# Projection tiles of a hybrid attention and mLSTM block computed in another order

## The reference, cut to what matters

```
h = rms_norm(x, mix_norm_w)
proj = h @ w_in
aq, ak, av, iq, ik, iw, mq, mk, mv, mi, mf, mo = split(proj)
# indexer: which 256 keys each query may see, for every block of 128 queries
idx_score = einsum('bqh,bqhs->bqs', wi, relu(einsum('bqhd,bsd->bqhs', qi, ki)))
sel = top_k(idx_score masked to earlier chunks, 256)
att_out = softmax(rope(aq) . rope(ak)[sel]) . av[sel]          # 8 heads, 2 key heads
# mLSTM: 4 heads of 128, chunkwise matrix memory
q, k = split(silu(causal_conv4([mq, mk])))
mem_out = norm(mlstm(q, k, mv, mi, log_sigmoid(mf))) * sigmoid(mo)
x = x + concat(att_out, mem_out) @ w_out
x = x + moe(rms_norm(x))                                       # top 4 of 32 experts
out = rms_norm(x)
```

## Time and profile before

| | |
|---|---|
| time, median of 3 runs | 2528.6 us (2527.76 to 2529.83) |
| the profiled execution's own time | 2529.42 us |
| its span, first to last instruction | 2527.6 us |
| PE busy | 2269.2 us (90%) |
| DVE busy | 1806.2 us (71%) |
| ACT busy | 1378.8 us (55%) |
| POOL busy | 520.3 us (21%) |

### The profile page before, as it was taken

The page is one execution under the profiler, slowest core; times in us unless marked ns, Lnnn a source line. Parts: engine busy times, 40 slices in busy tenths (PEclk is TensorE's granted clock), DMA queues, the critical chain, the costliest instruction groups (busy, mean ns, idle before and its releaser), DMA issues.

```text
span 2527.6 us, 41675 instructions
## 1 busy us (share of the span) xinstructions
PE 2269.2 (90%) x15519; PEld 1799.5 (71%) x15519; DVE 1806.2 (71%) x2070; ACT 1378.8 (55%) x1547; POOL 520.3 (21%) x455
## 2 busy tenths in 40 slices
PE   5689999757997949999999999999999999999994
PEld 4567788656886747777777777777777777777773
DVE  3589999904434378778778778678777777777885
ACT  3362223555653246666566566566666666656665
POOL 1006786670002001111110110111111111101020
PEclk9899999767998969999999999999999999999997
DMA  5011111001003338888798897898888888879887
GB/s 131 17 34 34 51 50 52 12 21 67 1 2 123 119 136 306 285 311 300 278 319 306 270 325 279 293 319 284 299 310 287 307 291 302 309 283 314 308 314 276
DMA packets 253391, 525.95 MB, mean 208 GB/s; under 512 B 32969, under 2 KB 59721, under 8 KB 252973
## 3 DMA queue, kind: packets, MB, share of 16 engines
q1 hardware_dynamic: 240204, 483.27, 53.8%
q0 software_dynamic: 13120, 41.82, 6.4%
HBM read 490.44 MB, written 35.91 MB: 208 GB/s over the span
## 4 chain that ended last, share of the span: by engine, by line
PE 72%; DMA 9%; DVE 6%; ACT 5%; issue 4%; POOL 2%; SPq 1%; POOLq 0%; ACTq 0%; DVEq 0%
PE ps L1701 13%; PE ps L1702 12%; PE ps L1703 12%; PE ps L1708 6%; PE ps L1400 6%; PE ps L1401 6%; PE ps L1402 6%; DMA xg<-h_d,gcur 5%; DMA e_raw<-in_w_gate_up_dram 3%; PE ps L1579 2%; PE ps L1713 1%; PE ps L1691 1%; PE ps L1570 1%; PE ps L1752 1%; DVE score L1921 1%
## 5 line engine op out<-in xcount | busy, mean ns | idle before, releaser
L2208 DVE TENSOR_TENSOR e_wlo<-e_raw,e_whi 128x2048 fp32r<-128x2048 f32 x410 | 925.3, 2284 | 143.8 <-ACT e_whi L1283 142.4
L1283 ACT ACTIVATE e_whi<-e_raw 128x2048 fp32r<-128x2048 f32 x411 | 783.6, 1915 | 371.0 <-PE ps L1703 212.2
L1701 PE MATMUL ps<-e_whi,xh 128*128 128x512 f32 x1088 | 441.9, 406 | 5.8 <-DVE e_wlo L2208 5.8
L1702 PE MATMUL ps<-e_whi,xl 128*128 128x512 f32 x1088 | 425.6, 391 | 0.0
L1703 PE MATMUL ps<-e_wlo,xh 128*128 128x512 f32 x1088 | 424.8, 390 | 0.0
L933 POOL DMA_INDIRECT x_d<-ym,scur x34 | 72.1, 2121 | 942.8 <-ACT ym L1316 923.1
L1701 PEld LDWEIGHTS ps<-e_whi,xh 128*128 128x128 f32 x1088 | 204.7, 188 | 71.2 <-issue 26.4
L1703 PEld LDWEIGHTS ps<-e_wlo,xh 128*128 128x128 f32 x1088 | 204.8, 188 | 44.9
L1702 PEld LDWEIGHTS ps<-e_whi,xl 128*128 128x128 f32 x1088 | 205.0, 188 | 37.7
L1701 PE MATMUL ps<-e_whi,ath 128*128 128x512 f32 x544 | 226.1, 416 | 6.2 <-DVE atl L2236 4.9
L1703 PE MATMUL ps<-e_wlo,ath 128*128 128x512 f32 x544 | 213.5, 392 | 0.0
(11 more groups left out here) (357 smaller groups left out, 3581.7 us busy)
## 6 DMA issues: line engine op xcount, KB each, us to landing
e_raw<-in_w_gate_up_dram SPq DMA_DIRECT2D x275, 1024.0 KB, 5.2
e_raw<-in_w_down_dram SPq DMA_DIRECT2D x136, 1024.0 KB, 7.8
w_raw<-in_w_in_dram SPq DMA_DIRECT2D x20, 512.0 KB, 3.8
xt<-in_x_dram SPq DMA_DIRECT2D x8, 512.0 KB, 3.5
wo_raw<-in_w_out_dram SPq DMA_DIRECT2D x8, 512.0 KB, 6.6
xr<-in_x_dram SPq DMA_DIRECT2D x8, 512.0 KB, 4.2
x_d<-x SPq DMA_DIRECT2D x8, 512.0 KB, 2.6
h_d<-h SPq DMA_DIRECT2D x8, 512.0 KB, 2.9
```

The lines of the kernel that those rows point to most:

```text
L1283: nc.scalar.activation(e_whi[:, m % HRING, :], e_raw[:, m % RING, :], ACT.Copy).then_inc(s.e_hi, 1)
L1701: nc.tensor.matmul(dst, a_hi, slot_hi, start=False, stop=False, skip_group_check=True)
L1702: nc.tensor.matmul(dst, a_lo, slot_hi, start=False, stop=False, skip_group_check=True)
L2208: nc.vector.tensor_tensor(e_wlo[:, m % HRING, :], e_raw[:, m % RING, :], e_whi[:, m % HRING, :].bitcast(F32), ALU.subtract).then_inc(s.e_l ...
```

## The change

Tiles 0 to 3 stay. The order behind them becomes: 4 to 7 mLSTM values, 8 to 15 convolved queries and keys, 16 to 19 output gates, 20 to 23 attention queries, 24 keys, 25 values.

- PE computes tile 4 behind the indexer's rotary swaps, then transposes the indexer weights, then computes tile 5, and only then begins the score units.
- Tiles 6 and 7 are cut into 16 parts of three matmuls. A part follows each even score unit from unit 8 on, 20 parts in all: the whole of tile 6 and four parts of tile 7. The other 12 parts of tile 7 follow the indexer. Tile 6 is evacuated by ACT behind Relu 42.
- The value tiles' transposes move from banks 0 to 3 to the banks 4 to 7 that held their tile: two in the first score block (behind units 1 and 3), the third behind the indexer, the fourth behind tile 8. A tile's PSUM banks are now also held by its transposes, so tiles 6 to 9 wait for the copies of tiles 4 to 7.
- The convolutions are done four operations to a tile in tiles 10 to 23, as before relative to their own tiles. The rotary turns of the attention tiles now come in POOL's queue at 22 to 26: the first two in front of the last eight convolution operations, the last one behind all tiles, and the attention value tile's evacuation, transposes and copy behind that.
- Buffers are placed anew (`vtmp`, `vmo`, `vwide`, `qtmp`), and SP stores the output gates in between the loads of tiles 19 to 22.

```diff
-FT_IQ, FT_IK, FT_SMALL, FT_Q, FT_K, FT_V, FT_MQK, FT_MV, FT_MO, NFT = 0, 2, 3, 4, 8, 9, 10, 18, 22, 26
+FT_IQ, FT_IK, FT_SMALL, FT_MV, FT_MQK, FT_MO, FT_Q, FT_K, FT_V, NFT = 0, 2, 3, 4, 8, 16, 20, 24, 25, 26
+PARTS = 16
+CONV_EACH = 4
...
# POOL
+                if f == FT_MV + 1:
+                    gp.wait_ge(s.v_gate, 12)
+                    gp.wait_ge(s.v_ra, 3)
+                    nc.gpsimd.memset(mvtok[:, :, :, MD:MD + 1], 1.0).then_inc(s.g_zero, 1)
...
-                if f >= FT_MQK + 2:
-                    for n in range(4 * (f - FT_MQK - 2), 4 * (f - FT_MQK - 1)):
+                if FT_MQK + 2 <= f < NFT:
+                    first = CONV_EACH * (f - FT_MQK - 2)
+                    for n in range(first, min(first + CONV_EACH, 8 * CONV_STEPS)):
                         convolve(n)
...
# ACT, inside the loop over the 48 score units
+                if u == 3:
+                    rows_of_values(0)
+                if u == 5:
+                    rows_of_values(1)
+                if u == 42:
+                    evacuate(FT_MV + 2)
+                    hi(FT_MV + 4)
...
# ACT, in the loop over the later tiles
+                for j in range(8):
+
+                    if FT_MQK + 2 + (CONV_STEPS * j + CONV_STEPS - 1) // CONV_EACH == f:
+                        silu(j)
+                if f <= NFT:
                     evacuate(f - 1)
...
# PE
+                if n == 0:
+                    pe.wait_ge(s.g_wlo, f + 1)
...
+                    if FT_MV + 2 <= f < FT_MQK + 2:
+                        pe.wait_ge(s.a_vt, f - FT_MV - 1)
...
+            project(FT_MV)
             pe.wait_ge(s.a_ev, 4)
             pe.wait_ge(s.v_rm, 3)
             for t in range(NT):
                 m = nc.tensor.transpose(ps[:, 0, t * IH:(t + 1) * IH], iwt[0:IH, t * P:(t + 1) * P], ident[0:IH, 0:IH])
             m.then_inc(s.p_iwt, 1)
+            project(FT_MV + 1)
             pe.wait_ge(s.a_iwt, 1)
             pe.wait_ge(s.v_iqlo, 1)
+            part = 0
...
                 m.then_inc(s.p_is, 1)
+                if u == 1:
+                    value_transposes(0)
+                if u == 3:
+                    value_transposes(1)
+                if u >= 8 and u % 2 == 0:
+                    project_part(FT_MV + 2 + part // PARTS, part % PARTS)
+                    part += 1
...
-            for f in range(4, NFT + 1):
+            value_transposes(2)
+            for f in range(FT_MV + 3, NFT + 1):
                 if f < NFT:
-                    project(f)
+                    project(f, part - PARTS if f == FT_MV + 3 else 0)
+                if f == FT_MQK:
+                    value_transposes(3)
```

More of the change, by code:

```diff
@@ new lines, in _, with iq_hi_of @@
+            hi(0)
+            for f in range(1, FT_MV):
+                hi(f)
+                evacuate(f - 1)
+            hi(FT_MV)
+            evacuate(FT_SMALL)
+            hi(FT_MV + 1)
+            act.wait_ge(s.v_ra, 3)
+            nc.scalar.activation(ik_hi[:], ikt[:], ACT.Copy).then_inc(s.a_iqhi, 1)
+            def iq_hi_of(i):
+                if i == 2:
+                    act.wait_ge(s.g_zero, 1)
+                if i >= 4:
+                    act.wait_ge(s.p_is, IH * (i - 3))
+                for g in range(4):
+                    rows = slice(ID * g, ID * g + ID)
+                    nc.scalar.activation(iq_hi[rows, i % 2, g::4, :], iqt[rows, :, i * P:(i + 1) * P], ACT.Copy).then_inc(s.a_iqhi, 1)
@@ new lines, in _ @@
+            iq_hi_of(2)
+            act.wait_ge(s.p_iwt, 1)
+            nc.scalar.activation(iwc, ps[:, 0, 0:NT * IH].rearrange("p (t h) -> p t h", t=NT), ACT.Copy).then_inc(s.a_iwt, 1)
+            evacuate(FT_MV)
+            hi(FT_MV + 2)
+            evacuate(FT_MV + 1)
+            hi(FT_MV + 3)
+            for u in range(6 * IH):
+                i, h = 2 + u // IH, u % IH
+                w = P * (i + 1)
+                if h == 2 and i + 1 < NT:
+                    iq_hi_of(i + 1)
+                act.wait_ge(s.p_is, u + 1)
+                if u >= 2:
+                    act.wait_ge(s.v_score, 9 * ((u - 2) // IH) + (u - 2) % IH + 1)
+                nc.scalar.activation(rbuf[:, u % 2, 0:w], pair(2 * (u % 2))[:, 0:w], ACT.Relu).then_inc(s.a_relu, 1)
+                if u == 3:
[5 more added lines that the diff above has]
+                    hi(FT_MV + 4)
@@ L1110, in m_chunk @@
+                if f == FT_V + 2:
+                    rows_of_values(4)
             def m_chunk(c):
```

176 lines of the change are left out of this document (77 added, 99 removed).

## The result

The changed kernel takes 2536.8 us (median of 9 runs, 2531.34 to 2543.53), the kernel before in the same session 2528.2 us (2527.14 to 2530.55): a ratio of 1.0034, 95% interval 1.0020 to 1.0047. It is slower, by 8.6 us, where I had said 2526 and most likely no difference; it lies outside my range of 2518.5 to 2535. Both intervals lie above 1, but differences of this size are small beside the spread of the times (2531.34 to 2543.53 above). The profiled execution took 2531.62 us, 5 us under the median; a second profile of the same kernel took 2539.01. I read both.

A forecast was written before the change was run, and what follows sets the result against it. PE was taken to bound the kernel up to the first mLSTM matmul, with some 32 us idle ahead of an all-PE stretch. Items 1 to 7 sum to -4.6, the clock adds +2.1, giving -2.5 us: 2526, range 2518.5 to 2535.

The forecast's parts named there:

- Item 1: Start of the scores, first block: unit 8 on PE at 125.8 instead of 123.2, +2.6 us.
- Item 2: Five score blocks with 20 parts partly filling PE's waits: +6.0 us; plus 0.9 for value transposes behind the indexer.
- the 0.9: One set of value transposes added behind the indexer: +0.9 us of PE work.
- Items 3, 4 and 5: PE work moved off the later tiles: -38.1 us; new wait between tiles 8 and 9, convolutions in tiles 10 to 21: nothing.
- Item 6: Attention tiles: POOL, with rotary turns and convolutions, makes PE wait 2.2, 4.7, 5.8 and 1.7 us: +14.4.
- Item 7: Tail: PE waits 10.8 us for the last turn, evacuations and copies, against 1.15 before: +9.6.
- Item 8: Granted clock falls around PE's waits in the attention tiles and tail: +2.1 us, bounds 0 and 11.
- my own case: Whole kernel: 2526 us, own range 2522 to 2530, with the clock costing +2.1; 56%.
- The second one (2535): PE falls to the low clock in first score block, tile 24 and tail, paying 11.3 us: 2535; chance 11%.
- The first: Score blocks: parts fit fully into PE's waits, blocks grow only +3.2 us, clock costs nothing: 2521; chance 24%.
- the third: POOL falls behind from tile 10 on, 12 tiles 0.9 us longer, +10.8: 2537; chance 7%.
- the fourth: Score blocks: PE alternating between two PSUM bank pairs runs half the time at half rate, +15 us: 2541; chance 2%.

The follow-up runs named there:

- apart: Changed kernel with POOL's low parts of tiles 7 and 8 held behind score additions and tile 6's put before the scores: 2532.9 us, 1.0011 to before.
- portop: Kernel before the change with three POOL operations added beside DVE's score additions, their results unused: 2528.4 us, one run.
- noparts: Changed kernel with no parts of tiles 6 and 7 between score units, both tiles following the indexer: 2542.3 us, 1.0049 to before.
- tail: Changed kernel with the attention value tile's buffer separated from the rotary turns' scratch, so its evacuation need not wait for the last turn: 2525.1 us, 0.9983 to before.
- warm: Changed kernel with nine unused matmuls filling PE's last wait, before the attention values' transposes: 2531.6 us, 1.0008 to before.
- again: Changed kernel run once more without any edit, for a second profile and set of times: 2535.1 us, 1.0019 to before.
- tailapart: Changed kernel with the value tile freed from the last turn and low parts of tiles 7 and 8 kept off the scores: 2527.6 us, 0.9985 to before.
- bestwarm: Changed kernel with separate tail buffers, later low parts, rotary turns on DVE, and two unused matmuls in the last wait: 2510.4 us, 0.9917 to before.

## Why the prediction was wrong, by its own steps

The sum was for the first mLSTM matmul, and said 435.6. Against the two profiles of the changed kernel (us):

| term | predicted | first profile | second |
|---|---|---|---|
| items 1 and 2, to the gates' transposes | +8.6 | +12.0 | +12.4 |
| items 2 (the 0.9), 3, 6, 7 and 8, from there to the instant | -11.1 | -11.8 | -10.0 |
| instant against before | -2.5 | +0.2 | +2.4 |
| first chunk, against 4.9 | 0 (in item 8) | +1.5 | +3.7 |
| `m_kw` to the end | 0 | +0.5 | +3.5 |
| sum | -2.5 | +2.2 | +9.6 |

- **Item 1 failed.** It put the cost of POOL's low parts beside DVE at nothing. The step was "by following the three engines through the eight units I get unit 8 on PE at 125.8 instead of 123.2: +2.6"; Relu 8 came 5.1 later (129.3 against 124.2). I followed DVE's additions at the durations of a trace in which POOL stood idle through the whole indexer (0.00 us of POOL), and the change puts POOL's low parts there. I counted them as time on POOL alone ("its low part is no obstacle"). They cost DVE 1.75 us at the rotary product, 3.4 at the first additions and 1.3 at an addition of 1024 keys in the last block; 3.4 to 3.8 us more than I had reached the gates' transposes. The first of the three did not count against my sum: DVE's first score came at 118.26, 0.7 before my 119.0. `apart` and `portop` show it, from both sides; `apart`, which takes away the second and the third but puts 2.1 us onto a scan and 0.9 onto another addition, gives 3.1 back. The trace before shows no such place in the indexer, but it has one behind the attention, which I did not look for: four low parts on DVE beside four on POOL, then two of the same size on DVE beside a memset of POOL. The Trainium skill (SBUF — State Buffer, "Who interferes with whom") lists this collision: a VectorE instruction with two SBUF inputs contends with a GpSimd instruction that reads SBUF for a shared port pair, which is an exclusive lock, and the order of issue decides which one is blocked. The numbers agree, to 0.1 us: POOL's low part ended at 97.64 + 2.39 = 100.03, and 1.21 behind that is 101.24; the product ended at 101.11. These are the rows of the kernel before (DVE twice, then POOL):

```profile
759.07 12.41 DVE L2023 TENSOR_TENSOR wo_lo<-wo_raw,wo_hi 128x1024 fp32r<-128x1024 f32 x4 [3.27 <-ACT wo_hi L1240]
771.41 2.35 DVE L2028 TENSOR_TENSOR mx_lo<-mixt,mx_hi 128x1024 fp32r<-128x1024 f32 x2
```
```profile
758.17 12.23 POOL L884 TENSOR_TENSOR wo_lo<-wo_raw,wo_hi 128x1024 fp32r<-128x1024 f32 x4 [186.32 <-ACT wo_hi L1240]
```

  Side by side, one takes 3.1 us on DVE and 3.1 on POOL; without the other, 1.2 and 2.4 (240.06 in the earlier trace rows). With these rows the collision could have stood in the prediction as a term or a rival.
- **Item 2** held but for that: from Relu 8 to Relu 47 the blocks grew by 6.9 us, not 6.0, and the last block's low part with its 1.3 is in that. `noparts` shows the parts' gain. (One reading ahead of it was off: the 1.2 us behind the last unit is not one of the ten waits of the earlier trace rows, so nine waits with 10.5 us lay in the blocks. No term changes by it.)
- **Items 3, 4 and 5** held: one wait of 1.3 for `mvtok`, none for a low part in tiles 10 to 21.
- **Item 6** held in mechanism, and in size as a whole. The rows of after, in the order in which I had followed them:

```profile
371.18 1.06 ACT L1054 ACTIVATE mqk<-ctmp 128x1024 f32<-128x1024 f32 x1 [8.50 <-POOL ctmp L770]
372.14 1.01 ACT L1042 ACTIVATE qt<-ps 128x1024 f32<-128x1024 f32 x1
...
373.20 3.67 PE L1540 MATMUL ps<-qt,cst 128*128 128x512 f32 x4 [1.97 <-ACT qt L1042]
...
379.94 0.61 PE L1429 MATMUL ps<-ht_hi,w_hi 128*128 128x512 f32 x1 [3.07 <-POOL w_lo L778]
...
394.34 1.06 ACT L1054 ACTIVATE mqk<-ctmp 128x1024 f32<-128x1024 f32 x1 [16.41 <-POOL ctmp L770]
...
396.37 2.95 PE L1540 MATMUL ps<-qt,cst 128*128 128x512 f32 x4 [3.65 <-ACT qt L1042]
```

  The waits are 2.0, 3.1, 3.7 and 0.5, together 9.2, against my 2.2, 4.7, 5.8 and 1.7, together 14.4. PE's own work filled the rest: a swap that takes 1.76 took 3.67 here, at a low clock. POOL's queue set the time, whatever PE did in it: from the first swap to the third I had 37.8 us, and it is 37.9 in both traces. Behind the third, where PE's own speed counts, tile 24 at the low clock took 0.5 us more than at the full one in the first trace and 2.3 more in the second.
- **Item 7** held: 9.5 us, and `tail` takes 7.5 of them away.
- **Item 8 was mis-sized.** I took +2.1, with bounds 0 and 11. In the tail alone `warm` measures 4.6, where I had "about 1 to 2". I had tied that loss to the 9.6 us of waiting; `tail` shows the first chunk as slow (8.6 us) behind a wait of 2.0. The clock fell in a third place too, which my own case had put at nothing: in the first block, where the low parts made PE wait 1.84 us for a Relu (0.80 and 0.88 in the windows). In `apart` that wait and that low clock are gone together; which brought which is not shown, and waits of up to 1.33 us are left there at a clock of 1.00.
- **The rivals.** The second one (2535) came closest to the medians, at 11%: the clock did fall in all three of its places, but the part of it that I can put a number to (0.5 to 2.3 in tile 24, 2.4 to 4.6 in the tail) is less than its 11.3, and the collision on DVE and POOL, which was no rival of mine, comes with up to 3.8. The first is refuted: it needed the blocks to grow by 3.2 us and the clock to cost nothing, and they grew by 6.9; the third by the missing waits; the fourth by windows of 1.00 with units and parts alternating. Of the signs I had set, the gates' transposes came 12.0 us later and not 8.5, and the first mLSTM matmul at 438.4 and 440.6 and not at 432 to 437. Of the conditions for being wrong, two came true: the clock was under 1.00 between 123 and 370, and in the second profile the work behind the first chunk differs by 3.5 us. The blocks of 512 to 1024 keys by themselves grew by 6.9, so that one did not. The top-k's room is 52.5 us, as expected (about 50 instead of 63.4):

```profile
DVE k_lo L2015 <- ACT k_hi L1227: 52.5, 1, 52.5
```

- **The whole.** Of the 12.1 us between my sum and the second profile (9.6 + 2.5), 3.8 lie up to the gates' transposes, where `apart` and `portop` point to POOL's low parts (with the clock that fell behind them), 1.1 from the rest of the projection, 3.7 from the first chunk at the low clock, and 3.5 from behind it, for which no step of mine and no edit gives a cause. The first profile is off by 4.7: 3.4, -0.7, 1.5 and 0.5. The medians lie between the two.
- **What stays open.** From the first token transposes of the experts to the end the profiles differ by up to 6 us (1595.3 to 1601.7) with no relation to the edits: 3 of the 9.6 us of the second profile lie there. Why the low clock of tile 24 lasts longer in some executions is open as well, and so is what makes the first chunk fall to it: it took 6.2 us (`noparts`) to 8.6 (`again`) behind waits of 9.5, and 6.2 (`tailapart`) to 8.6 (`tail`) behind waits of 2.0.

## What to carry to other kernels

Before moving work to an idle engine, ask what the engine beside it reads at that moment: durations in a trace hold only for the neighbours they had, and here a POOL instruction added its own rest to a DVE instruction on the path. A wait of PE can cost more than its length, since the work behind it can run at half the clock, here also behind waits of 2.0 us; price it with that, or fill it with matmuls that nobody reads, as long as nothing queues behind them. Such a gain in the trace need not reach the time: it did not in `bestwarm`. And when a reordering gives back its gain, look for the two or three places where it was given back: moving the five rotary turns, one buffer and a few low parts made the same order 25 us faster.
